# Side work of the projections on other steps: gate weights and decay logarithms, four modulation chunks, retention's decay tables

## What is computed

```python
mod = c_act @ w_ada[l] + b_ada[l]                    # first block: shift, scale, gate
h = rmsnorm(x, norm_g[l]) * (1.0 + scale[:, None]) + shift[:, None]
proj = h @ w_in[l]       # im, fm: the gates, 8 of its columns, read by mlstm_chunkwise
lam = exp(sum(lam_q1 * lam_k1)) - exp(sum(lam_q2 * lam_k2)) + lam_init   # for diff_attention
...
sh1, sc1, g1, sh2, sc2, g2 = _modulation(c, w_ada[i], b_ada[i])          # second block
log_gf = jax.nn.log_sigmoid(ret_decay_logit[i, 0])   # and log_gb: the decay rates
s_f, s_b = _context_states(kc, vc, log_gf, log_gb)   # weights exp(log_g * distance to the end)
yx, _, _ = _bidir_retention(qx, kx, vx, log_gf, log_gb, s_f, s_b)        # scores * exp(log_g * |i - j|)
x = x + g1 * _rms_norm(mix_x, post_mix_g[i])
hx2 = _rms_norm(x, pre_ffn_g[i]) * (1.0 + sc2) + sh2
ffn_x = _expert_choice_ffn(hx2, w_router[i], b_router[i], w_gate[i], w_up[i], w_down[i])
x = x + g2 * _rms_norm(ffn_x, post_ffn_g[i])
```

## Time and profile before

| | us |
|---|---|
| median of three runs | 1554.63 |
| lowest and highest run | 1553.75, 1555.62 |
| the profiled execution's own time | 1552.24 |
| its span in the profile | 1550.4 |
| PE busy in the span | 1203.9 (78%) |
| DVE busy | 612.1 (39%) |
| ACT busy | 428.1 (28%) |

### The profile page before, as it was taken

One profiled execution on the slowest core, in us unless ns is written; L12 is line 12 of the kernel. 1 busy time (PEld: TensorE's weight loads), 2 busy tenths in 40 slices (PEclk: granted clock), 3 DMA queues, 4 the chain that ended last, 5 costly groups with the idle time before them and its releaser, 6 DMA issues.

```text
span 1550.4 us, 18202 instructions
## 1 busy us (share of the span) xinstructions
PE 1203.9 (78%) x7368; PEld 695.5 (45%) x7368; DVE 612.1 (39%) x1037; ACT 428.1 (28%) x648; POOL 36.9 (2%) x62
## 2 busy tenths in 40 slices
PE   7999999999999999976565665666655664666675
PEld 5888977887888899721111111111111211111122
DVE  3786789889777876511011011011011011010111
ACT  3665357786564674300000000000000000000001
POOL 0100000010001000000000000000000000000000
PEclk9999999999999999988877877877887788777778
DMA  9876867687756666999999999999999999999996
GB/s 363 284 262 214 312 240 247 237 302 241 265 203 199 217 218 259 386 427 432 431 432 432 432 432 432 429 429 432 431 431 432 431 429 430 431 429 432 431 432 278
DMA packets 78323, 550.62 MB, mean 355 GB/s; under 512 B 5032, under 2 KB 5320, under 8 KB 61856
## 3 DMA queue, kind: packets, MB, share of 16 engines
q1 hardware_dynamic: 75168, 541.08, 86.3%
q0 software_dynamic: 2784, 8.08, 1.7%
q10 hardware_dynamic: 288, 0.30, 0.1%
HBM read 548.36 MB, written 1.61 MB: 355 GB/s over the span
## 4 chain that ended last, share of the span: by engine, by line
PE 46%; DMA 35%; DVE 11%; ACT 4%; issue 3%; SPq 0%; DVEq 0%; ACTq 0%; POOL 0%
PE ps L610 43%; DMA b<-in_w_down 34%; DVE b L1535 5%; PE ps L614 3%; ACT b L1171 2%; DVE b L1552 2%; DVE b L2260 1%; ACT b L1173 1%; DVE b L2201 1%; DMA b<-in_w_in 1%; DMA b<-in_w_ada 1%; DVE b L2207 1%; DVE b L1545 0%; DVE b L1566 0%; DVE b L2239 0%
## 5 line engine op out<-in xcount | busy, mean ns | idle before, releaser
L610 PE MATMUL ps<-b,b 128*32 128x512 f32 (+7 forms) x6922 | 1136.1, 545 | 292.7 <-DMA b<-in_w_up 115.5
L610 PEld LDWEIGHTS ps<-b,b 128*32 128x32 f32 (+2 forms) x6922 | 639.8, 160 | 749.5 <-issue 451.7
L1171 ACT ACTIVATE b<-ps 128x512 f32<-128x512 f32 (+3 forms) x165 | 92.2, 559 | 868.3 <-PE ps L610 569.9
L1535 DVE TENSOR_TENSOR b<-b,b 128x1024 fp32r<-128x1024 f32 (+5 forms) x254 | 277.0, 1091 | 98.5 <-ACT b L1171 79.5
L1171 ACT ACTIVATE b<-b 128x1024 fp32r<-128x1024 f32 (+6 forms) x219 | 219.1, 1001 | 209.1 <-PE ps L610 175.4
L2250 DVE TENSOR_TENSOR b<-b,ps 128x512 f32<-128x512 f32 x16 | 11.0, 687 | 392.9 <-issue 353.0
L2260 DVE TENSOR_TENSOR b<-b,ps 128x1024 f32<-128x1024 f32 x28 | 34.2, 1221 | 306.7 <-PE ps L610 306.7
L614 PE MATMUL ps<-b,b 128*128 128x128 f32 (+1 forms) x360 | 69.0, 320 | 38.5 <-DVE b L1566 23.5
L614 PEld LDWEIGHTS ps<-b,b 128*128 128x128 f32 (+1 forms) x360 | 45.4, 166 | 89.2 <-DVE b L1566 36.3
L1552 DVE SCALAR_TENSOR_TENSOR b<-b,b,b 128x512 f32<-128x512 f32 (+3 forms) x50 | 63.1, 1263 | 4.3 <-ACT b L1171 0.5
L1535 DVE TENSOR_TENSOR b<-ps,b 128x512 f32<-128x512 f32 (+8 forms) x69 | 37.6, 545 | 27.0 <-PE ps L610 15.5
(11 more groups left out here) (59 smaller groups left out, 201.2 us busy)
## 6 DMA issues: line engine op xcount, KB each, us to landing
b<-in_w_up SPq DMA_DIRECT2D x30, 4096.0 KB, 43.2
b<-in_w_gate SPq DMA_DIRECT2D x29, 4096.0 KB, 43.0
b<-in_w_down SPq DMA_DIRECT2D x29, 4096.0 KB, 38.5
b<-in_w_in SPq DMA_DIRECT2D x73, 1024.0 KB, 5.3
b<-in_w_ada SPq DMA_DIRECT2D x28, 1024.0 KB, 5.2
b<-in_w_gate SPq DMA_DIRECT2D x6, 2048.0 KB, 9.0
b<-in_w_down SPq DMA_DIRECT2D x5, 2048.0 KB, 14.0
b<-in_w_ada SPq DMA_DIRECT2D x16, 512.0 KB, 11.5
```

Source lines behind the costliest of these rows:

```text
L610: return e.matmul(o, lhsT, rhs, start=start, stop=stop, skip_group_check=True)
L1171: e.activation(o, i, f, bias=bias, scale=scale).then_inc(mark[0], 1)
L1535: e.tensor_tensor(o, a, b, op).then_inc(mark[0], 1)
```

## The change

The four last chunks of the second modulation (24 to 27) move from steps (21, 1), (22, 1), (23, 1) and (25, 3) to (28, 1), (28, 4), (28, 7) and (29, 2); the sum of R4 from (26, 0) to (29, 4) and its `mod_rows` from (26, 1) to (29, 5). The split of the gates' weights stays at (2, 1), with nothing of the logarithms ahead of it; logarithms and `lam` move to (7, 1) and (7, 2). `WT` moves on DVE from (29, 1) to (29, 4) to all four steps of s = 33, `wfb` from (29, 5) to (34, 0), the exponentials on ACT from (29, 6) to (34, 1), the scaling of `wfb` from (29, 7) to (34, 2). ACT waits at (30, 1) for R4's rows, because the buffer that it writes there holds their bias until then. Nothing is computed otherwise.

```diff
@@ -163,10 +163,10 @@
 ADA_STEP = {(a + 1, 3): a for a in range(NADA_PE)}
 for _a, _step in enumerate(((9, 0), (9, 2), (10, 0), (10, 2), (11, 0), (11, 2), (12, 0), (12, 3),
                             (13, 3), (14, 3), (15, 3), (16, 3),
-                            (17, 3), (18, 3), (19, 3), (20, 3), (21, 1), (22, 1), (23, 1), (25, 3))):
+                            (17, 3), (18, 3), (19, 3), (20, 3), (28, 1), (28, 4), (28, 7), (29, 2))):
     ADA_STEP[_step] = [ADA_STEP[_step], NADA_PE + _a] if _step in ADA_STEP else NADA_PE + _a
 ADA_AT = {step: a if isinstance(a, list) else [a] for step, a in ADA_STEP.items()}
-ADA_SUM = {(13, 0): "R3", (17, 0): "R2", (26, 0): "R4"}
+ADA_SUM = {(13, 0): "R3", (17, 0): "R2", (29, 4): "R4"}
 RING = 4
 LOADS = []
 
@@ -1284,12 +1284,13 @@
 
 
                 if (s, c) == (2, 1):
+                    e.wait_ge(S("few_in"), 48)
+                    copy(WIF[0], wif, to=S("a_wif"))
+                if (s, c) == (7, 2):
                     e.wait_ge(S("v_ls1"), 1)
                     act(lt1, lt1, ACT.Exp, scale=-1.0, to=S("a_ls1"))
                     e.wait_ge(S("v_lam"), 1)
                     act(lamv, lamv, ACT.Exp, to=S("a_lam"))
-                    e.wait_ge(S("few_in"), 48)
-                    copy(WIF[0], wif, to=S("a_wif"))
 
 
                 if s in (2, 4, 6, 8):
@@ -1380,6 +1381,8 @@
                         act(CJ, CXN[:, t, :], ACT.Square, accum=csq[:, t:t + 1], to=S("a_xsq"))
                 if s == 30 and c or (s, c) == (31, 0):
                     q = c - 1 if s == 30 else 3
+                    if q == 0:
+                        e.wait_ge(S("v_modt"), 2)
                     if q >= 2:
                         e.wait_ge(S("v_mod"), q + 3)
                     modulate_hi(f"CF{q}", CTH, GSC, SHC)
@@ -1408,7 +1411,7 @@
                     rows("CK", lambda t: KC[:, t, :])
                 if (s, c) == (36, 0):
                     rows("CV", lambda t: VC[:, t, :])
-                if (s, c) == (29, 6):
+                if (s, c) == (34, 1):
                     for h in range(RH):
                         e.wait_ge(S("v_wt"), h + 1)
                         act(WT[:, h, :], WT[:, h, :], ACT.Exp)
@@ -1807,13 +1810,15 @@
                     modulate_lo("XT3", 1, HTL, HTH)
 
 
-                if (s, c) == (2, 0):
-                    e.wait_ge(S("few_in"), 48)
+                if (s, c) == (2, 1):
+                    e.wait_ge(S("a_wif"), 1)
+                    tt(WIF[1], wif, WIF[0].bitcast(F32), ALU.subtract, to=S("v_wif"))
+                if (s, c) == (7, 1):
                     logs_first(lg, lt1, S("v_ls1"))
                     tt(l4[:, 0:4:2, :], l4[:, 0:4:2, :], l4[:, 1:4:2, :], ALU.mult)
                     reduce(lamv, l4[:, 0:4:2, :], ALU.add, to=S("v_lam"))
                     ts(ag, part(cols, COLS, "anorm_g"), 1.0 - LAM_INIT, None, ALU.mult)
-                if (s, c) == (2, 1):
+                if (s, c) == (7, 2):
                     e.wait_ge(S("a_ls1"), 1)
                     for i in range(3):
                         logs_rest(lgs, lg, lt1, lt2, i)
@@ -1821,8 +1826,6 @@
                     e.wait_ge(S("a_lam"), 1)
                     tt(lamv[:, 0:1], lamv[:, 1:2], lamv[:, 0:1], ALU.subtract)
                     ts(neglam, neglam, LAM_INIT, None, ALU.subtract)
-                    e.wait_ge(S("a_wif"), 1)
-                    tt(WIF[1], wif, WIF[0].bitcast(F32), ALU.subtract, to=S("v_wif"))
 
 
                 if s in (4, 6, 8) and c < 3:
@@ -1880,7 +1883,7 @@
                     mod_rows(1, "R3", MODT[2])
                 if (s, c) == (17, 1):
                     mod_rows(2, "R2", MODT[1])
-                if (s, c) == (26, 1):
+                if (s, c) == (29, 5):
                     mod_rows(3, "R4", MODT[0])
                 for a in ADA_AT.get((s, c), ()):
                     if a >= NADA_PE:
@@ -2021,9 +2024,9 @@
                     modulate(f"XF{2 * c - 1}", GS2, SH2)
                     for q in (2 * c - 2, 2 * c - 1):
                         modulate_lo(f"XF{q}", 9, HTL, HTH)
-                if s == 29 and 1 <= c < 5:
-
-                    h = c - 1
+                if s == 33:
+
+                    h = c
                     if h == 0:
                         e.wait_ge(S("late_in"), 16)
                     ts(WT[:, h, :], part(late, LATE, "ahead"), lgs[:, h:h + 1], None, ALU.mult)
@@ -2044,7 +2047,7 @@
                         e.wait_ge(*free(n))
                     reduce(vmean[:, i, :], (VC4, VX4)[i], ALU.add)
                     ts(vmean[:, i, :], vmean[:, i, :], -1.0 / RD, None, ALU.mult, to=S("v_vm"))
-                if (s, c) == (29, 5):
+                if (s, c) == (34, 0):
                     for d in range(2):
                         for t in range(NT):
                             ts(wfb[:, d, t, :], lgs[:, d * RH:(d + 1) * RH], wn[:, d, t:t + 1], None, ALU.mult,
@@ -2053,7 +2056,7 @@
                     for n in ("K2a", "K2b"):
                         e.wait_ge(*free(n))
                     rotary(KX, "cosx", "sinx", c - 1)
-                if (s, c) == (29, 7):
+                if (s, c) == (34, 2):
                     e.wait_ge(S("a_wfb"), 1)
                     ts(wfb, wfb, RD ** -0.5, None, ALU.mult)
                 if (s, c) in ((36, 2), (36, 3)):
```

## The result

The kernel after takes 1556.87 us (median of 20 runs, 1556.28 to 1561.11), the kernel before, beside it on the same chip, 1553.82 us (20 runs, 1551.54 to 1557.26). The ratio is 1.0024 with a 95% interval of 1.0018 to 1.0029, which is 3.7 us slower (2.8 to 4.5); the two medians themselves lie 3.05 us apart.

The account below looks back on a forecast made before the run. PE was taken to bound the projections, DMA the experts' stream from 645 us. Table and exponential costs of 6.2 us less gains of 1.6 gave +4.6 on 1554.63, so 1559.2 us, range 1552.8 to 1561.5.

Parts of the forecast that it names:

- Gates' weights: At 62 us, with the logarithms no longer ahead of the split, PE's wait of 0.95 us goes entirely.
- Logarithms at cost 0: At (7, 1) and (7, 2), DVE's 3.01 us of idle time covers the logarithms; with the cover gone 4.2 us.
- Chunks: Moved to (28, 1) to (29, 2): PE's 0.32 us at 360.8 go; cost 0, with half the cover gone 2 us.
- DVE's tables: At step 33 and (34, 0): they delay the low half of (35, 0), so PE stands still 3.6 us longer.
- ACT's exponentials: At (34, 1): table load and five exponentials; the high half at 505.97 moves 7.1 us, leaving 6.2 us on PE at 544.
- PE's second wait: Behind the flips, after PE's longer wait ahead of (35, 0): a second bracket on PE of about 1 us.
- No drain: At (34, 1): the table load costs only its 1.28 us; the documented drain of about 1.38 us was left out.
- Rival D: Behind (34, 1), the table load's drain lies on DVE's chain: 1.4 us more, 1560.6; chance 0.03.
- A: DVE's new work at (33, 2) to (34, 0) is hidden in idle time: 1553.0, or 1551.3 without half clock; chance 0.20.
- B: PE loses 3.6 us at 506; DVE and ACT regain the rest by 544: 1556.6; chance 0.16.
- E: At (29, 4) or (30, 1), chunk 27 or its rows come too late and PE waits: 2.7 us, 1561.9; chance 0.03.
- C: Behind PE's wait of some 4.5 us at (35, 0), the clock falls to half: +3.4 us, 1562.6; chance 0.05.

Follow-up runs that it names:

- g_gates: Kernel before with only the gates' split and the logarithms moved as in the change; ratio 0.9997 (0.9986 to 1.0008).
- x_clock: Kernel after with ACT's exponentials at (35, 3) to (37, 0) and 18 matmuls without use ahead of half (35, 0); ratio 1.0009 to the kernel before.
- b_logs11: Kernel after with DVE's tables at (30, 3) to (33, 1), exponentials at (34, 0), logarithms at (11, 0) to (12, 0); ratio 1.0007 to the kernel before.
- t_tables: Kernel before with only the decay tables (WT and wfb, DVE's and ACT's parts) moved to (33, 0) to (34, 2); ratio 1.0041 (1.0028 to 1.0055).
- c_clock: Kernel after with 18 matmuls without use ahead of half (35, 0); profiled once, not timed: 4.0 us behind the kernel before at (39, 0).
- x_explate: Kernel after with ACT's exponentials moved to (35, 3) and (36, 1) to (37, 0), DVE's tables unchanged; ratio 1.0015 to the kernel before.
- b_logs2: Kernel after with DVE's tables at (30, 3) to (33, 1), exponentials at (34, 0), logarithms at (2, 1), (2, 2); ratio 0.9992 to the kernel before.
- e_nogates: Kernel before with chunks moved, DVE's tables at (30, 3) to (33, 1), exponentials spread over (33, 2) to (34, 0); ratio 0.9988 (0.9976 to 1.0001).
- e_logs2: Kernel after with DVE's tables at (30, 3) to (33, 1), exponentials over (33, 2) to (34, 0), logarithms at (2, 1), (2, 2); ratio 0.9986 to the kernel before.

## Why the prediction was right, and where only its sum was

The range (1552.8 to 1561.5) holds 1556.87, and the likeliest case, slower by over 0.2%, came, though the interval reaches down to 0.18%. The sum was +4.6 us; measured are +3.7 (2.8 to 4.5). The time itself lies 2.3 us below the forecast 1559.2 and 0.6 below its likely part: 0.8 of that because the three runs that the forecast started from (1554.63) were above the median of twenty (1553.82), the rest because the sum was too high. Its steps:

1. **Gates' weights: right.** -1.2 us on PE, bracket gone.
2. **Logarithms at cost 0: wrong, the one step of the sum that failed.** They cost 1.1 us at 143. The cover that I named, DVE's 3.01 us at 132.00, is there in some executions only. It stood right behind the stretch at half clock at 126.9 to 130.3: DVE waited for ACT, and ACT for a PE that was 1.5 us slow. Where that stretch is missing (the profiles of the kernel after and of g_gates), the reserve is smaller and PE waits. Where it comes, the cover holds: in x_clock, whose clock is at half from 126.5 to 129.9, there is no bracket at 143. Nor is there one in b_logs11, with the gates' lead and without the half clock, but with the logarithms elsewhere: the wait needs both. And the score tables, which stood ahead of that idle time, now come behind the logarithms. DVE in the kernel after:

```profile
127.18 1.37 DVE L1555 SCALAR_TENSOR_TENSOR b<-b,b 128x8 f32<-128x8 f32 x7
...
129.52 0.29 DVE L1538 TENSOR_TENSOR b<-ps,b 128x128 f32<-128x128 f32 x1
...
131.54 1.23 DVE L1538 TENSOR_TENSOR b<-b,b 128x1024 fp32r<-128x1024 f32 x1
...
142.43 0.56 DVE L1555 SCALAR_TENSOR_TENSOR b<-ps,b 128x384 f32<-128x384 f32 x1
```

The last row is what PE waits for at 143.13. Between the first rows and it DVE has no bracket.
3. **Chunks: nearly right in size, incomplete in kind.** -0.9 us for 0.32 and its surplus of up to 0.3. One high half was late by 1.5 us (ACT's bracket 3.14 in place of 1.66, for `in_w_proj_a`), inside the 1 to 2 us given for it, and PE didn't notice. What I missed is that the chunks at 21 to 25 pin PE to DVE, so that they decide about every lead made earlier (g_gates).
4. **DVE's tables: right.** The low half of (35, 0) was to be 3.6 us late; against PE's own shift it is 506.26 - 504.78 + 2.2 = 3.7.
5. **ACT's exponentials: right.** Load and exponentials stand where they were put, the high half at 505.97 became 510.87 (+7.1 with the lead), that at 510.88 became 515.76 (+7.1). The sum of both was +6.2, measured 6.2 (5.9 in t_tables). PE's second wait, 0.9 us behind the flips, didn't come in the kernel after, since half clock filled its time; in c_clock it did, 0.99. At the place of 544 2 us were expected, and 0.40 measured, 1.48 in c_clock: the same reason.
6. **No drain: right.** The exponentials start at 507.65, 0.02 us behind a load of 1.28 us. The 1.38 us that the Trainium skill, page "ScalarE: Activation LUTs", section "What ACT_TABLE_LOAD costs", adds show in none of these rows. Rival D falls.

**The sum.** Gains of 1.6 were predicted. In the profile they are 2.2 at (34, 0): 1.2 (gates) + 1.5 (the missing half clock of 126.9) - 1.1 (the wait at 143) - 0.3 (a bracket of 0.16 at 267, which all kernels with the split ahead have except b_logs11, and for which I found no cause) + 0.9 (chunks). Where that half clock fell too, in x_clock, they are 1.9. The cost being 6.2, the profiles give +4.0 to +4.3, inside the interval of the runs; the sum's 4.6 was 0.3 to 0.6 too high because its gains, 1.6, were too small.

That the gains came out near 1.6 all the same is in part luck. The half clock that fell ahead of the kernel before's reading and not in the after's gave 1.5 us that no term of the sum has, against 1.1 and 0.3 lost in places where the sum has nothing. g_gates suggests why this chance counts for the kernel after at all and not for the one before: with the chunks at 21 to 25 a lead of 1.4 us is lost by 361 us. A profile of the kernel before without that half clock would show it, and none was taken.

Of the rivals, A and B fell (4.53 us at (35, 0); 6.2 us still there at (39, 0)), E didn't occur. **C happened and cost nothing.** The clock fell to 0.50 for 6.8 us, from 505.80 on, when PE had stood still for 2.7 us of the wait that ended at 507.63. Its price (+3.4) was wrong: it set a loss of 5.1 us against 1.7 in hand. The loss was 2.3 (twelve matmuls of 5.29 us for 2.98) or little more, since PE stood still for the first 1.8 us of the stretch, and in hand were the 0.99 + 1.48 = 2.5 us that PE waits in c_clock. The Trainium skill, page "TensorE: Matmul & The Clock Gate", section "What's actually happening", says that the clock follows how busy PE has recently been; the three long waits agree with it, while the stretch near 127 us, under unbroken work of PE, shows no such cause.

## What to carry to other kernels

An idle time that is meant to cover new work must be read together with the clock of the stretch ahead of it: a wait behind half clock is not there in every execution. Where two engines hand work to each other, gains made ahead of a stretch in which PE is pinned to the slower one are lost there, so free that stretch first and measure the parts together. And work of several instructions that need nothing of a norm should stand ahead of the norm's chain, in waits that the other engine has anyway (here 3.3 us on ACT with DVE's tables early), spread over more than one where one is too short: DVE's tables moved in this way and ACT's exponentials spread turned 6.2 us of cost into 0.1. Before such a wait is used, take out of it what the change itself has made longer.

## What the runs showed of the hardware

In the projections waits of 4.17, 4.52 and 4.53 us on PE went with half clock (1.2 for 2.4 GHz) for 3.4, 6.8 and 6.8 us (t_tables, x_explate, after), in all three profiles that had so long a wait. The clock fell 0.3, 0.8 and 1.8 us before the wait was over. The shorter waits, up to 2.81 us (b_logs11), had none, and the clock stayed full over the matmuls without use that took 4.2 us of the same place. But a stretch of 3.4 us at half clock also came near 127 us under unbroken work of PE, in four of the fourteen profiles (before, t_tables, x_clock, b_logs2), and one of 3.4 or 6.8 us near 645 us in nine. What decides whether these two come isn't shown. The busy rows of t_tables behind its wait and of x_clock near 127:

```profile
510.00:513.40 3.40, 3.07 (x7) 2.51 (x8) 2.02 (x5) 3.02 (x6) 1.31 (x2) 0.50 0.02 5
```

```profile
126.50:129.90 3.40, 3.40 (x18) 3.40 (x18) 2.75 (x16) 0.25 (x2) 0.00 (x0) 0.50 0.88 282
```

The one near 127 us is worth 1.5 us: b_logs11, e_nogates and e_logs2, which have neither it nor a wait there, gain 1.5 us on the kernel before between 121 and 155 us. One profile of each kernel is few: where two profiles differ by 1.5 us, such a stretch is the first thing to look for.
